# S5 products by lag with operands exchanged, four tiles in four column groups and one transposition back; VectorE's scans ahead of the pads of lags

## The chip, the cores and the metric

One core of one Trainium2 chip runs the whole program. The metric is the device time of one execution in microseconds, and the time of a kernel is the median of its runs. TensorE does matrix products, VectorE and ScalarE elementwise work (both read PSUM), GpSimd elementwise work in SBUF, SyncE issues most transfers.

## The reference

The reference is one inference step of a two-layer trunk, for a prompt of 256 tokens and 8 single tokens. Layer 0 is gated linear attention with a short convolution and a dense SwiGLU; layer 1 is an S5 state-space mixer and a mixture of eight experts. The edited code belongs to the S5 mixer:

```python
u = (h @ w_in).reshape(bsz, t, S5_GROUPS, S5_GROUP)        # 64 groups of 16 channels
bu = einsum('btgi,gpi->btgp', u, bb)                       # complex, 64 states a group
x_t = ab * x_{t-1} + bu_t                                  # for each group and state
y = einsum('gip,btgp->btgi', c_re, x_re) - einsum('gip,btgp->btgi', c_im, x_im) + d_skip * u
```

Everything is float32.

## The kernel before

Every engine has its own list of instructions, written out by hand, and runs it in order; semaphores tie the lists together. The S5 mixer takes four time steps as one, so that the recurrence runs over 64 chunks (`CHUNKS`) of 4 steps. Two groups fill 128 partitions with their 2 x 64 states, and such a pair is one of 32 pairs; the kernel works on 4 pairs at a time, in 8 tiles `k` of 4 pairs `r`. Within a chunk the output of one step from the input of an earlier one needs only the product of C, A to the power of the lag, and B: a 16x16 matrix for each group and each lag 0 to 3. These are the products by lag.

For each tile `k`:

- ScalarE's `pad_b` (L1097) lays the 4 lags of B of each pair in `b_pad`, 128 partitions (2 groups x 64 states) by 128 columns (4 lags x 2 groups x 16 inputs), with zeros where state and input belong to different groups.
- TensorE's `turns_of_b` (L2238) transposes the 8 blocks (4 pairs, real and imaginary) into banks 6 and 7, and ScalarE's `b_mats` (L1119) copies them out.
- TensorE's `lag_products` (L2248) multiplies, for each pair, `b_pad` as the stationary operand with C (`c_now`, 16 columns) as the moving one, real and imaginary part into one sum: bank 3 then holds 128 rows (lag, group, input) by 16 outputs for each pair.
- VectorE's `lags` (L1714) masks this into `k_pad` (L1720) and adds the skip term in four small instructions (L1725); ScalarE's `k_mats` (L1126) spreads it into `k_mat`.
- TensorE's `chunk_sums` (L2258) makes the input of the recurrence, `turn_back` (L1693) on VectorE and two additions on GpSimd (L786, L787) rotate it, `scans` (L1730) runs it over the chunks with two scan instructions, and `rotate_im` (VectorE) and `rotate_re` (GpSimd, L769) rotate back.
- GpSimd's `pad_c` (L757) pads C, `sample_states` (L1138) and `last_states` (L1147) copy states on ScalarE.
- TensorE's `outputs` (L2270) sums `k_mat` times the input and padded C times the states into bank 4, and ScalarE's `gelu` (L1154) takes it out.

The four lists run these steps of different tiles in a loop over `k`. TensorE: transposes of tile k+1, outputs of tile k-2, products by lag and chunk sums of tile k+1. VectorE: `turn_back` of k, `lags` of k+1, `scans` and `rotate_im` of k-1. GpSimd: decay and additions of k, `pad_c` of k, `rotate_re` of k-1. ScalarE: `b_mats` of k+1, `pad_b` of k+2, `sample_states` and `k_mats` of k, `last_states` of k-1, `gelu` of k-2. `pad_c` and `k_mats` of a tile write into buffers that `outputs` two tiles earlier still reads, so they wait for it. In the first rounds and near the end TensorE also makes pieces of the modulation (`ada`, L1975): products of 32 stationary columns (`csT`) and 512 moving ones, in four column groups of the array, which write to four quarters of the partitions.

All products go through one helper, `mm` (L1938), so in the profile they carry line 1939 and are told apart by their operands: products by lag read `arena,plain_hi`, chunk sums `arena,plain_lo` in 16 passes, outputs `arena,plain_lo` and `plain_parts,plain_hi` in turn. A float32 product is two MATMUL records. Transposes are line 2245.

Of the kernel before, what the change touches and what calls it, by code (L numbers as in the profile page):

```python
# [7 lines left out]
ALU = mybir.AluOpType  # L8
ACT = mybir.ActivationFunctionType
# [5 lines left out]
P = 128  # L15
D = 1024
KT = D // P
# [105 lines left out]
def hybrid_trunk(nc, x_prompt, x_sample, c_prompt, c_sample, state_gla, state_conv, state_s5_re, state_s5_im,  # L123
# [11 lines left out]
    with ExitStack() as ctx:  # L135
# [5 lines left out]
        def sem(name):  # L141
            return ctx.enter_context(nc.semaphore(name))
# [49 lines left out]
        def shaped(flat, shape):  # L192
            if len(shape) == 2:
                return flat.rearrange("p (a b) -> p a b", b=shape[1])
            if len(shape) == 3:
                return flat.rearrange("p (a b c) -> p a b c", b=shape[1], c=shape[2])
            return flat
# [8 lines left out]
        def bview(ap, shape, *dims):  # L206

            for d in dims:
                ap = ap.unsqueeze(d)
            return ap.broadcast_to(shape)  # L210
# [65 lines left out]
        b_mat = [shaped(x[:, 0:1024], (2, 4, P)) for x in mats]  # L276
        k_mat = [shaped(x[:, 1024:1536], (4, 4, QUAD)) for x in mats]
        k_pad = [shaped(x[:, 1536:1664], (4, QUAD)) for x in mats]
        work = [shaped(plain_parts[:, 1024 * i:1024 * i + 1024], (4, 4, CHUNKS)) for i in range(2)]
        x_in = [shaped(plain_parts[:, 2048 + 584 * i:2632 + 584 * i], (2, 4, CHUNKS + NS + 1)) for i in range(2)]  # L280
        decay = [shaped(plain_parts[:, 3216 + 256 * i:3472 + 256 * i], (4, CHUNKS)) for i in range(2)]
# [3 lines left out]
        def two(at, *shape):  # L285
# [81 lines left out]
            sem(n) for n in ("steps_ready", "c_now_ready", "turns_ready", "table_ready", "table_saved",  # L367
                             "cos_loaded", "sin_loaded", "u_cleared", "k_cleared",
                             "u_first", "u_second"))
        b_pad_ready, c_pad_ready, tr_full, b_mat_ready, k_full, k_pad_ready, k_mat_ready = (  # L370
            sem(n) for n in ("b_pad_ready", "c_pad_ready", "tr_full", "b_mat_ready", "k_full", "k_pad_ready",
                             "k_mat_ready"))
        w_full, w_used, w_ready, z_ready, xre_ready, xim_ready, xs_ready, y_full, y_used, y_moved = (
            sem(n) for n in ("w_full", "w_used", "w_ready", "z_ready", "xre_ready", "xim_ready", "xs_ready", "y_full",
# [488 lines left out]
        def _(act):  # L863
# [233 lines left out]
            def pad_b(k):  # L1097

                if k >= 2:
                    act.wait_ge(tr_full, k - 1)  # L1100
                    act.wait_ge(k_full, k - 1)
                for i in range(2):
                    for g in range(2):
                        ins = act.activation(b_pad[k % 2][:, i, :, :].rearrange("q r (s g i) -> q (r s) g i", g=2, i=16)[:, :, g, :],
                                             b_steps[i][:, 4 * k:4 * k + 4, :, :].rearrange("q r s i -> q (r s) i"),
                                             ACT.Copy, scale=half_rows[:, g:g + 1])
                ins.then_inc(b_pad_ready, 1)
# [11 lines left out]
            def b_mats(k):  # L1119

                act.wait_ge(tr_full, k + 1)
                for i in range(2):
                    ins = act.activation(b_mat[k % 2][:, i, :, :].rearrange("q r p -> q (r p)"), bank[6 + i][:, :], ACT.Copy)
                ins.then_inc(b_mat_ready, 1)

            def k_mats(k):  # L1126

# [31 lines left out]
                act.activation(y_one[:, k, :, :], out[:, :, 0:NS], ACT.Gelu_apprx_tanh).then_inc(y_used, 1)  # L1159

            b_mats(0)
            act.wait_ge(acc_full, TILES["in1"] + KT)
            pad_b(1)
            for k in range(KT + 2):
                if k + 1 < KT:
                    b_mats(k + 1)
                if k + 2 < KT:
                    pad_b(k + 2)
                if k in (1, 2):
                    act.wait_ge(u_cleared, 1)  # L1170
                    for s_ in range(4):
                        act.activation(*place(slice(4, 8), k + 1, s_), ACT.Copy)
                    for at, s_ in ((0, 0), (CHUNKS + NS, 3)):
                        ins = act.activation(u_in[QUAD * s_:QUAD * s_ + QUAD, 4:8, k + 1, at:at + NS],
                                             uT[QUAD * (k + 1):QUAD * (k + 1) + QUAD, 4:8, TP:T], ACT.Copy)
                    if k == 2:
                        ins.then_inc(u_second, 1)
                if k < KT:
                    sample_states(k)
                    k_mats(k)  # L1180
                if k < 3:
                    ada(17 + k)
                if 1 <= k <= KT:
                    last_states(k - 1)
                if k >= 2:
                    gelu(k - 2)
                if k == KT:
                    ada(20)
                    split_dense_hi(act, 42)
# [121 lines left out]
        def _(dve):  # L1311
# [3 lines left out]
            def step(ins):  # L1315

                count[0] += 1
                ins.then_inc(v_step, 1)
                dve.wait_ge(v_step, count[0])
# [394 lines left out]
            def lags(k):  # L1714


                dve.wait_ge(k_full, k + 1)
                if k >= 2:
                    dve.wait_ge(k_mat_ready, k - 1)
                step(dve.tensor_tensor(k_pad[k % 2].rearrange("q r (g o) -> q r g o", g=2),  # L1720
                                       bview(bank[3][:, 0:64].rearrange("q (r o) -> q r o", r=4), [P, 4, 2, 16], 2),
                                       bview(group_mask[:, :], [P, 4, 2, 16], 1, 3), ALU.mult))
                last = k_pad[k % 2][96:P, :, :]
                for r in range(4):
                    ins = dve.scalar_tensor_tensor(out=last[:, r, :], in0=ident[96:P, 96:P],  # L1725
                                                   scalar=d_col[96:P, 4 * k + r:4 * k + r + 1], in1=last[:, r, :],
                                                   op0=ALU.mult, op1=ALU.add)
                ins.then_inc(k_pad_ready, 1)
# [9 lines left out]
            def rotate_im(k):  # L1738

                wk, x = work[k % 2], x_in[k % 2][:, 1, :, NS + 1:]  # L1740
                dve.wait_ge(z_ready, 2 * k + 2)
                if k >= 2:
                    dve.wait_ge(y_full, k - 1)
                    dve.wait_ge(last_copied, k - 1)
                dve.tensor_tensor(x, turn_sin[:, k, :, :], wk[:, 0, :, :], ALU.mult)
                step(dve.tensor_tensor(wk[:, 3, :, :], turn_cos[:, k, :, :], wk[:, 2, :, :], ALU.mult))
                dve.tensor_tensor(x, x, wk[:, 3, :, :], ALU.add).then_inc(xim_ready, 1)

            lags(0)
            for k in range(KT + 1):  # L1750
                if k < KT:
                    turn_back(k)
                if k + 1 < KT:
                    lags(k + 1)
                if k:
                    scans(k - 1)
                    rotate_im(k - 1)
                if 1 <= k <= 3:
                    mod_rows(16 + k)
                if k >= KT - 1:  # L1760
                    dve.wait_ge(y_used, 4)
                    for r in (2 * k - 14, 2 * k - 13):
                        for s_ in range(4):
                            dve.tensor_copy(*from_chunks(slice(0, 4), r, s_))
# [168 lines left out]
        def _(pe):  # L1933
# [4 lines left out]
            def mm(out, lhsT, rhs, start, stop):  # L1938
                return pe.matmul(out, lhsT, rhs, start=start, stop=stop, skip_group_check=True)  # L1939
# [307 lines left out]

            def lag_products(k):  # L2248

                if k:  # L2250
                    pe.wait_ge(k_pad_ready, k)
                for r in range(4):
                    for i in range(2):
                        ins = mm(bank[3][:, 16 * r:16 * r + 16], b_pad[k % 2][:, i, r, :], c_now[:, i, 4 * k + r, :],
                                 i == 0, i == 1)
                ins.then_inc(k_full, 1)

            def chunk_sums(k):  # L2258

                pe.wait_ge(b_mat_ready, k + 1)  # L2260
                pe.wait_ge(*((u_first, 1) if k < 4 else (u_second, 2)))
                if k:
                    pe.wait_ge(w_used, k)
                n = CHUNKS + NS
                for i in range(2):
                    for r in range(4):
                        ins = mm(bank[1 + i][:, n * r:n * r + n], b_mat[k % 2][:, i, r, :], u_in[:, k, r, NS:], True, True)
                ins.then_inc(w_full, 1)
# [17 lines left out]
            turns_of_b(0)  # L2286
            lag_products(0)
            chunk_sums(0)
            for k in range(KT + 2):
                if k + 1 < KT:  # L2290
                    turns_of_b(k + 1)
                if k >= 2:
                    outputs(k - 2)
                if k + 1 < KT:
                    lag_products(k + 1)
                    chunk_sums(k + 1)
                if 1 <= k <= 3:
                    ada_rows(16 + k)
                if k < 3:
                    ada(17 + k)  # L2300
                if k == KT:
                    ada(20)
# [231 lines left out]
```

## Time and profile before

| | |
|---|---|
| median of 3 runs | 1842.84 us (1841.28 to 1846.24) |
| profiled execution | 1847.72 us, span 1845.9 us, mean granted clock 0.943 |
| busy share of the span | TensorE 94%, VectorE 75%, ScalarE 65%, GpSimd 8% |
| chain that ended last | TensorE 84%, VectorE 6%, issue 4%, DMA 3%, GpSimd 1%, ScalarE 2% |
| the S5 rounds with the edited code | about 506 to 637 us of the span |

How it is read: times are microseconds from the start of the span. A busy time counts an engine's own instructions; PEld is TensorE's loading of stationary operands, which overlaps PE. The clock is the share of full speed that was granted to TensorE: 1.00 is 2.4 GHz, 0.50 is 1.2 GHz. In an answer, `out<-in` names the memory written and read; `plain_hi`, `plain_lo`, `plain_parts` and `arena` are areas of SBUF, `bank` is PSUM. What stands in brackets at the end of a row is how long the engine was idle before it and what ended that. Ends of matmuls are modelled.

### The profile page before, as it was taken

How to read it: one execution, taken by the hardware profiler on the slowest of the kernel's cores; microseconds unless marked ns; L12 is line 12 of the kernel's file. 1: busy time of each engine (PE TensorE's matmuls, PEld its weight loads, DVE VectorE, ACT ScalarE, POOL GpSimd, SP SyncE). 2: the span in 40 equal slices, each digit the busy share in tenths (PEclk: the TensorE clock that was granted, in tenths of full speed). 3: DMA queues.
4: the chain of work that ended last, by engine and by line, in shares of the span. 5: the costliest groups of instructions: out<-in, count | busy, mean ns of one | idle time of the engine just before them, and what ended most of it. 6: DMA issues, size and time to landing. Idle time of an engine off the chain costs nothing.

```text
span 1845.9 us, 27103 instructions
## 1 busy us (share of the span) xinstructions
PE 1734.2 (94%) x9191; PEld 1457.0 (79%) x9191; DVE 1379.5 (75%) x1579; ACT 1201.8 (65%) x1491; POOL 146.4 (8%) x199
## 2 busy tenths in 40 slices
PE   6988899998899797999999999999999999999994
PEld 3877799986779695887887878878878788788884
DVE  3564445491643736998998989989989899899997
ACT  3623355303463445878888888888888888888885
POOL 1041000000044300700000000000000000000001
PEclk8988999999865698999999999999999999999997
DMA  8662654335630249998998989989989899899995
GB/s 349 257 258 90 237 194 160 141 151 194 289 137 1 103 178 382 399 418 323 422 367 348 410 312 419 392 325 420 360 358 400 314 422 380 343 412 355 399 376 197
DMA packets 72903, 553.49 MB, mean 300 GB/s; under 512 B 8256, under 2 KB 8527, under 8 KB 15328
## 3 DMA queue, kind: packets, MB, share of 16 engines
q1 hardware_dynamic: 69186, 538.54, 73.9%
q0 software_dynamic: 3072, 12.54, 1.8%
q10 hardware_dynamic: 542, 1.20, 0.2%
q8 instruction: 43, 0.70, 0.1%
q14 instruction: 60, 0.49, 0.1%
HBM read 530.74 MB, written 21.53 MB: 299 GB/s over the span
## 4 chain that ended last, share of the span: by engine, by line
PE 84%; DVE 6%; issue 4%; DMA 3%; ACT 2%; POOL 1%; ACTq 0%; DVEq 0%; POOLq 0%; SPq 0%
PE bank L1939 81%; PE bank L2406 1%; DMA ring<-in_dense_rows_dram 1%; DVE w_lo L516 1%; DMA arena<-in_state_conv_dram 1%; DVE arena L1686 1%; ACT w_hi L511 1%; DVE sq L1364 0%; PE bank L2385 0%; DVE rstd L1346 0%; ACT w_hi L463 0%; DVE w_lo L469 0%; DMA fT<-y_rows,row_i 0%; DVE sq L1517 0%; DVE arena L1899 0%
## 5 line engine op out<-in xcount | busy, mean ns | idle before, releaser
L1939 PE MATMUL bank<-w_hi,parts 128*128 128x512 f32 x3024 | 899.0, 392 | 14.8 <-DVE w_lo L516 13.3
L516 DVE TENSOR_TENSOR w_lo<-ring,w_hi 128x1024 fp32r<-128x1024 f32 x654 | 782.4, 1221 | 81.1 <-PE bank L1939 29.8
L511 ACT ACTIVATE w_hi<-ring 128x1024 fp32r<-128x1024 f32 x654 | 690.7, 1062 | 157.4 <-PE bank L1939 157.3
L1939 PEld LDWEIGHTS bank<-w_hi,parts 128*128 128x128 f32 x3024 | 561.6, 188 | 134.1 <-DVE w_lo L516 18.6
L1939 PE MATMUL bank<-w_lo,parts 128*128 128x512 f32 x1512 | 548.3, 390 | 0.0
L1939 PE MATMUL bank<-parts,w_hi 128*128 128x264 f32 x1600 | 312.6, 297 | 21.9 <-DVE parts L1353 21.9
L1939 PEld LDWEIGHTS bank<-w_lo,parts 128*128 128x128 f32 x1512 | 283.9, 188 | 60.3
L1939 PEld LDWEIGHTS bank<-parts,w_hi 128*128 128x128 f32 x1600 | 260.6, 198 | 33.9 <-issue 21.5
L1939 PE MATMUL bank<-parts,w_lo 128*128 128x264 f32 x800 | 234.0, 293 | 0.0
L469 DVE TENSOR_TENSOR w_lo<-ring,w_hi 128x2048 fp32r<-128x2048 f32 x50 | 114.5, 2295 | 148.2 <-ACT w_hi L463 148.2
L1939 PEld LDWEIGHTS bank<-parts,w_lo 128*128 128x128 f32 x800 | 158.0, 198 | 0.0
L511 ACT ACTIVATE w_hi<-hT 128x1024 fp32r<-128x1024 f32 x108 | 114.5, 1061 | 36.5 <-PE bank L1939 36.4
L886 ACT ACTIVATE arena<-bank 128x264 f32<-128x264 f32 (+2 forms) x89 | 34.6, 390 | 156.1 <-PE bank L1939 156.1
L516 DVE TENSOR_TENSOR w_lo<-hT,w_hi 128x1024 fp32r<-128x1024 f32 x108 | 131.1, 1220 | 5.4
L463 ACT ACTIVATE w_hi<-ring 128x2048 fp32r<-128x2048 f32 x50 | 95.1, 1908 | 8.0 <-PE bank L1939 5.3
L1939 PE MATMUL bank<-arena,ring 128*128 128x264 f32 x352 | 81.7, 395 | 6.1 <-DMA ring<-in_dense_rows_dram 6.1
L857 POOL DMA_INDIRECT arena<-y_rows,row_i x4 | 3.8, 942 | 1045.1 <-DMA y_rows<-arena 1044.2
L1939 PEld LDWEIGHTS bank<-arena,ring 128*128 128x128 f32 x352 | 68.3, 195 | 19.4 <-issue 7.3
L898 ACT ACTIVATE sq<-bank 128x264 f32<-128x264 f32 x16 | 6.2, 390 | 82.3 <-PE bank L1939 82.3
L1939 PE MATMUL bank<-ring,csT 128*32 128x512 f32 x384 | 56.5, 710 | 2.6 <-DMA ring<-in_dense_rows_dram 2.6
L1939 PE MATMUL bank<-arena,plain_lo 128*128 128x72 f32 x192 | 42.5, 374 | 10.1 <-ACT arena L1159 10.1
L1875 DVE TENSOR_TENSOR parts<-bank,parts 128x512 fp32r<-128x512 f32 x63 | 43.1, 684 | 8.2 <-ACT parts L1258 8.2
(412 smaller groups left out, 1289.4 us busy)
## 6 DMA issues: line engine op xcount, KB each, us to landing
ring<-in_expert_rows_dram SPq DMA_DIRECT2D x330, 1024.0 KB, 7.2
ring<-in_dense_rows_dram SPq DMA_DIRECT2D x48, 2048.0 KB, 8.3
hT<-in_expert_rows_dram SPq DMA_DIRECT2D x55, 1024.0 KB, 7.2
ring<-in_dense_rows_dram SPq DMA_DIRECT2D x8, 1408.0 KB, 6.4
x_rows<-arena SPq DMA_DIRECT2D x1, 7168.0 KB, 28.8
y_rows<-arena SPq DMA_DIRECT2D x10, 512.0 KB, 6.6
arena<-x_rows SPq DMA_DIRECT2D x9, 512.0 KB, 8.1
ring<-in_dense_rows_dram SPq DMA_DIRECT2D x2, 1024.0 KB, 4.8
```

The source lines that it names most:

```text
L463: act.activation(hi, raw, ACT.Copy).then_inc(hi_ready, 1)
L469: dve.tensor_tensor(lo, raw, hi.bitcast(F32), ALU.subtract).then_inc(lo_ready, 1)
L511: act.activation(hi_slots[u % AHEAD], raw_unit(u), ACT.Copy).then_inc(hi_ready, 1)
L516: dve.tensor_tensor(lo_slots[u % AHEAD], raw_unit(u), hi_slots[u % AHEAD].bitcast(F32), ALU.subtract).then_inc(lo_ready, 1)
L857: pool.indirect_dma_start(to, None, y_rows, bass.IndirectOffsetOnAxis(row_i[0:rows, i, b:b + 1], 0))\
L886: act.activation(out, tile_bank(tile[0])[0:rows, 0:n], func, **more).then_inc(acc_free, 1)
L898: act.activation(sq[:, k, :], src, ACT.Square).then_inc(sq_ready, 1)
L1686: dve.tensor_copy(*place(ks, r, s_))
L1875: dve.tensor_tensor(h_t[c % 2][1], bank[6][:, :], h_t[c % 2][0].bitcast(F32), ALU.subtract)\
L1939: return pe.matmul(out, lhsT, rhs, start=start, stop=stop, skip_group_check=True)
L2406: ins = pe.transpose(bank[6][:, P * q:P * q + P], h_act[:, c % 2, P * q:P * q + P], ident[:, :])
```

## The change

The products by lag exchange their operands: C of two neighbouring pairs (2 x 16 = 32 columns) is stationary, and `b_pad` (128 columns) moves. Each of the 4 pairs `r` writes to its own quarter of bank 3's partitions, so that its product stands in its own column group of the array; of the 32 rows written, 16 belong to pair `r` and 16 to its neighbour's C, which are not used. The result is the transpose of what it was. So ScalarE copies it out of PSUM (`copy_lags`) into a new area `lag_rows`, TensorE transposes it back with one transposition (`turn_lags`) into other columns of bank 3, and VectorE's `lags` reads it there, in two instructions of half the size, since of every two neighbouring blocks it takes the first for even and the last for odd pairs. In TensorE's order the products by lag of tile k+1 now stand ahead of the outputs of tile k-2, and the turning back behind the chunk sums. In VectorE's order `scans` and `rotate_im` of tile k-1 now stand ahead of `lags` of tile k+1.

```diff
+        lag_rows = [x[:, 1664:1792] for x in mats]
...
 def pad_b(k):
     if k >= 2:
         act.wait_ge(tr_full, k - 1)
-        act.wait_ge(k_full, k - 1)
+        act.wait_ge(lag_full, k - 1)
...
+def copy_lags(k):
+    act.wait_ge(lag_full, k + 1)
+    if k >= 2:
+        act.wait_ge(k_full, k - 1)
+    act.activation(lag_rows[k % 2], bank[3][:, 0:P], ACT.Copy).then_inc(lag_copied, 1)
...
             b_mats(0)
+            copy_lags(0)
...
                 if k + 1 < KT:
                     b_mats(k + 1)
+                    copy_lags(k + 1)
                 if k + 2 < KT:
                     pad_b(k + 2)
...
 def lags(k):
     dve.wait_ge(k_full, k + 1)
     if k >= 2:
         dve.wait_ge(k_mat_ready, k - 1)
-    step(dve.tensor_tensor(k_pad[k % 2].rearrange("q r (g o) -> q r g o", g=2),
-                           bview(bank[3][:, 0:64].rearrange("q (r o) -> q r o", r=4), [P, 4, 2, 16], 2),
-                           bview(group_mask[:, :], [P, 4, 2, 16], 1, 3), ALU.mult))
+    for pair in range(2):
+        of_pair = bank[3][:, P + 64 * pair:P + 64 * pair + 64].rearrange("q (x o) -> q x o", o=16)[:, 0:4:3, :]
+        ins = dve.tensor_tensor(k_pad[k % 2][:, 2 * pair:2 * pair + 2, :].rearrange("q r (g o) -> q r g o", g=2),
+                                bview(of_pair, [P, 2, 2, 16], 2),
+                                bview(group_mask[:, :], [P, 2, 2, 16], 1, 3), ALU.mult)
+    step(ins)
...
                 if k < KT:
                     turn_back(k)
-                if k + 1 < KT:
-                    lags(k + 1)
                 if k:
                     scans(k - 1)
                     rotate_im(k - 1)
+                if k + 1 < KT:
+                    lags(k + 1)
...
 def lag_products(k):
     if k:
         pe.wait_ge(k_pad_ready, k)
-    for r in range(4):
-        for i in range(2):
-            ins = mm(bank[3][:, 16 * r:16 * r + 16], b_pad[k % 2][:, i, r, :], c_now[:, i, 4 * k + r, :],
-                     i == 0, i == 1)
-    ins.then_inc(k_full, 1)
+    for i in range(2):
+        for r in range(4):
+            pair = c_now[:, i, 4 * k + r // 2 * 2:4 * k + r // 2 * 2 + 2, :].rearrange("q t o -> q (t o)")
+            ins = mm(bank[3][QUAD * r:QUAD * r + QUAD, 0:P], pair, b_pad[k % 2][:, i, r, :], i == 0, i == 1)
+    ins.then_inc(lag_full, 1)
+
+def turn_lags(k):
+    pe.wait_ge(lag_copied, k + 1)
+    pe.transpose(bank[3][:, P:2 * P], lag_rows[k % 2], ident[:, :]).then_inc(k_full, 1)
...
             turns_of_b(0)
             lag_products(0)
             chunk_sums(0)
+            turn_lags(0)
             for k in range(KT + 2):
                 if k + 1 < KT:
                     turns_of_b(k + 1)
+                    lag_products(k + 1)
                 if k >= 2:
                     outputs(k - 2)
                 if k + 1 < KT:
-                    lag_products(k + 1)
                     chunk_sums(k + 1)
+                    turn_lags(k + 1)
```

## Rows read from the trace of the kernel before

**Rows 1.** Busy time of each engine by stretch (instructions), clock, DMA share, GB/s.
```profile
512.87:563.03 50.16, 49.11 (x280) 39.69 (x281) 23.71 (x66) 29.64 (x79) 23.76 (x29) 0.64 0.34 126
563.03:606.92 43.89, 40.07 (x186) 39.15 (x186) 17.71 (x47) 14.35 (x47) 19.82 (x24) 0.50 0.00 0
```

**Rows 2.** Waits from 505 to 637 us: total, times, longest.
```profile
DVE plain_lo L1720 <- PE bank L1939: 47.1, 7, 9.7
...
PE bank L1939 <- ACT arena L1159: 10.1, 5, 5.2
```

**Rows 3.** Chain that ended last, one round: start, us, what.
```profile
592.32 8.70 PE bank L1939 x40
...
601.05 0.30 DVE plain_lo L1720
...
602.16 1.29 DVE plain_parts L1735 x2
...
603.52 0.97 POOL plain_parts L776
...
606.21 0.21 ACT arena L1151
...
606.92 5.38 PE bank L1939 x24
```

**Rows 4.** Timeline of one late round: start, us, engine, instruction, count.
```profile
582.87 3.53 PE L1939 MATMUL bank<-arena,plain_hi 128*128 128x16 f32 x16
583.16 1.04 POOL L763 TENSOR_TENSOR plain_hi<-plain_hi,half_rows 128x512 f32<-128x512 f32 x1 [2.97 <-PE bank L1939]
...
586.24 3.67 PE L1939 MATMUL bank<-arena,plain_lo 128*128 128x72 f32 x16
...
589.70 1.92 PE L2245 MATMUL bank<-ident,plain_hi 128*128 128x128 f32 x8
...
592.07 1.09 ACT L1123 ACTIVATE plain_lo<-bank 128x512 f32<-128x512 f32 x2
```

**Rows 5.** Timeline of the early rounds, columns as in rows 4.
```profile
512.87 3.60 PE L1939 MATMUL bank<-arena,plain_hi 128*128 128x16 f32 x16 [0.27 <-DVE plain_lo L1725]
...
514.18 0.32 DVE L1709 TENSOR_TENSOR arena<-arena,bank 128x32 f32<-128x32 f32 x2
...
524.98 1.86 PE L1939 MATMUL bank<-arena,plain_hi 128*128 128x16 f32 x16
...
549.83 0.41 PE L1939 MATMUL bank<-arena,plain_lo 128*128 128x72 f32 x2 [1.05 <-ACT arena L1159]
```

**Rows 6.** Stretches by granted clock, columns as in rows 1.
```profile
511.04:524.69 13.65, 13.38 (x62) 9.88 (x61) 7.22 (x26) 5.29 (x15) 6.94 (x9) 0.50 0.06 13
524.69:528.10 3.41, 3.41 (x33) 3.41 (x31) 1.16 (x6) 2.87 (x7) 0.46 (x1) 1.00 0.78 308
...
534.90:541.75 6.85, 6.85 (x64) 6.85 (x62) 1.66 (x6) 6.27 (x16) 2.38 (x3) 1.00 0.83 307
```

**Rows 7.** Timeline around one piece of the modulation.
```profile
517.64 2.34 PE L1939 MATMUL bank<-arena,plain_lo 128*128 128x72 f32 x10
...
519.91 3.64 PE L1939 MATMUL bank<-ring,csT 128*32 128x512 f32 x16
...
520.76 0.20 PEld L1939 LDWEIGHTS bank<-ring,csT 128*32 128x32 f32 x4 [0.66 <-issue]
...
521.62 0.20 PEld L1939 LDWEIGHTS bank<-ring,csT 128*32 128x32 f32 x4 [0.66 <-issue]
...
523.48 0.48 PE L2245 MATMUL bank<-ident,plain_hi 128*128 128x128 f32 x1
```

**Rows 8.** Groups by line and shape, 563.03 to 606.89 us: busy us, mean ns.
```profile
L1158 ACT ACTIVATE arena<-bank 128x256 f32<-128x256 f32 x3 | 1.1, 367 | 0.0
...
L1709 DVE TENSOR_TENSOR arena<-arena,bank 128x32 f32<-128x32 f32 x6 | 0.9, 199 | 0.0
...
L1159 ACT ACTIVATE arena<-bank 128x32 f32<-128x32 f32 x3 | 0.6, 189 | 0.0
```

More of the change, by code:

```diff
@@ L369, in hybrid_trunk @@
                              "u_first", "u_second"))
-        b_pad_ready, c_pad_ready, tr_full, b_mat_ready, k_full, k_pad_ready, k_mat_ready = (
-            sem(n) for n in ("b_pad_ready", "c_pad_ready", "tr_full", "b_mat_ready", "k_full", "k_pad_ready",
+        b_pad_ready, c_pad_ready, tr_full, b_mat_ready, lag_full, lag_copied, k_full, k_pad_ready, k_mat_ready = (
+            sem(n) for n in ("b_pad_ready", "c_pad_ready", "tr_full", "b_mat_ready", "lag_full", "lag_copied", "k_full", "k_pad_ready",
                              "k_mat_ready"))
```

## The prediction

> **What bounds the kernel now.** I read the stage in which the edited lines run, by stretches, by waits, along the chain and instruction by instruction, in that order. The stretches say where TensorE is the limit: from 512.87 to 563.03 us it is busy 49.11 of 50.16 us, and from there to 606.92 us it is busy 40.07 of 43.89 us at the lower of its two clock levels, 1.2 GHz (granted 0.50) [rows 1]. The waits say who suffers: VectorE waits 47.1 us in seven pieces for TensorE before the first instruction of `lags` (L1720), and TensorE 10.1 us in five pieces for the gelu of ScalarE (L1159) [rows 2].
>
> The chain joins the two into a loop of 14.6 us that repeats once per tile of four groups [rows 3]: TensorE 8.70 us (`outputs`, then the products by lag), VectorE's pads from 601.05, its scans from 602.16, GpSimd's `rotate_re` from 603.52, ScalarE's `last_states` and gelu from 606.21, and TensorE again at 606.92. The scans need nothing from the products by lag; they only stand behind `lags` in VectorE's order. So one tile's scan waits for the next tile's products, and these wait behind `outputs`.
>
> What TensorE pays is a price per pass, not per column. A float32 product is two passes: 16 passes with 16 moving columns take 582.87 to 586.24, 16 with 72 columns take 586.24 to 589.70 [rows 4], together 6.83 us for 32, or 0.213 us each at 1.2 GHz, 0.107 at 2.4 GHz (the 16 passes of a tile in the stretch from 524.69 at granted 1.00 take 1.86 us with their tail [rows 5, 6]). What both have in common is 128 stationary columns.
>
> **The change part by part.**
>
> *Products by lag.* Before: 8 products, 16 passes of 128 stationary and 16 moving columns, 3.41 us at 1.2 GHz, 1.71 at 2.4. After: the same 16 passes with 32 stationary and 128 moving columns, in four column groups. The nearest rows are the modulation's products, in the same four groups with 512 moving columns: 16 passes, which start in waves of four, the third weights 0.86 us after the second (520.76, 521.62) [rows 7], at granted 0.50 [rows 6]. A wave of 512 columns in 0.855 us makes 0.213 us with 128, so four waves are 0.85 us. Entering and leaving the groups costs a little: ten passes from 517.64 would end at 519.77 and the modulation starts at 519.91, 0.14 us later; its four waves end at 519.91 + 3.42 = 523.33 and the transposes start at 523.48, 0.15 us later [rows 7]. So a tile costs 0.85 + 0.29 = 1.15 us at 1.2 GHz. At 2.4 GHz the waves are 0.43; the two switches lie between 0.15 and 0.30, I take 0.20, so 0.63. Bounds: four waves without switches (0.85) and no overlap at all (3.41 + 0.29 = 3.70).
>
> The Trainium skill (TensorE: Matmul & The Clock Gate, Part 3, measured speedups) puts three column tiles at 2.38 times instead of 3. The rows show whole waves of four; by the page's ratio a wave would take 0.27 instead of 0.213 us, and the sum below would be some 1.5 us smaller.
>
> *Turning back.* ScalarE's copy of 128x128 out of PSUM lies between its copies of 128x32 and 128x256, 0.19 and 0.37 us [rows 8]; I take 0.28. TensorE's transposition is one pass, 0.21 us at 1.2 GHz, 0.11 at 2.4. It waits for the copy, and behind it in TensorE's order stand the next tile's transposes and everything after. But the copy follows `b_mats`, done some 1.5 us after the transposes before it (589.70 + 1.92 = 591.62; `b_mats` 592.07 to 593.16 [rows 4]), while TensorE comes to the transposition only after products by lag, outputs and chunk sums, 1.15 + 5.12 + 3.41 = 9.7 us after those transposes. ScalarE would have to be 8 us late, so I cost the wait at nothing.
>
> *Pads of lags.* One VectorE instruction of 128x128 (0.30 us in the chain [rows 3]) becomes two of half the size; a small one out of PSUM, 128x32, is 0.20 us [rows 8]. So `lags` grows from 1.11 (601.05 to 602.16 [rows 3]) by between 0 and 0.3 us; I take 0.2. TensorE hides this: from the turning back to the next products by lag it has nine passes, 1.92 us, and the answer comes after 0.21, a pass's tail of 0.16 (582.87 + 3.53 against 586.24 [rows 4]) and 1.31 of `lags`, 1.7 us. At 2.4 GHz that cover is gone, and TensorE would wait about 0.6 us.
>
> *Scans ahead.* `scans` and `rotate_im` of the tile before now follow `turn_back` at once, and `rotate_re` no longer waits for them. VectorE is busy 17.71 of 43.89 us [rows 1], so there is room. What is late next on that side is GpSimd: `pad_c` waits for `outputs` and `rotate_re` stands behind it. That loop is 5.12 (outputs) + 0.29 to its start (582.87 to 583.16) + 2 x 1.04 [rows 4] + 2.69 (603.52 to 606.21) + 0.71 (to 606.92) [rows 3] = 10.9 us.
>
> *Three late rounds (563.03 to 606.92).* TensorE alone now needs 24 + 16 + 1 + 8 = 49 passes, 10.45 us, and 1.15 for the products by lag: 11.6 us, more than GpSimd's 10.9. Two rounds become 11.6; the third has neither transposes nor products by lag behind it and falls to GpSimd's 10.9. From 43.9 to 34.1: 9.8 us. If GpSimd and VectorE slow each other, 1 us a round less; if every round falls to GpSimd's loop, 1.4 more.
>
> *Early rounds (512.87 to 563.03).* TensorE is full, so its passes count one for one where nothing else is late. Tiles 1 to 4 had 3.41 + 1.71 + 1.71 + 3.41 = 10.2 us of products by lag. Now tiles 1 to 5 stand here, 1.15 + 0.63 + 0.63 + 1.15 + 1.15, with four turnings back of 0.64 in all: 5.35. That is 4.9 us less. The idle 1.05 us at 549.83, for a gelu behind a table load, is filled by tile 4's products, which now stand ahead of that wait [rows 5]: 5.9. Tile 1's chunk sums wait for `turn_back`, which ended at 514.50 and comes 0.2 later, where TensorE would be free at about 514.2 [rows 5]: 5.4. Other engines may be late in places I can't see; I take 5.0, bounds 2.5 and 6.
>
> *Before 512.87 and after 606.92.* Before it TensorE waits for VectorE anyway [rows 5]. After it there are no products by lag, and `scans` already stands first. Nothing in either.
>
> *The clock.* It stands at 2.4 GHz for 3.41 us from 524.69, a little after the modulation's 512-column passes, and falls after a stretch that holds tile 2's products with 16 moving columns; it comes up again for 6.85 us from 534.90 [rows 6]. With 128 columns in that place it may hold for another stretch after each of three such blocks. A stretch of 3.41 us at 2.4 GHz does up to 6.8 us of the same passes, so the bounds are 0 and 10 us; I take 2, near the rows in which it fell again.
>
> Sum: 9.8 + 5.0 + 2 = 16.8 us. The profiled execution took 1847.72 us (span 1845.9), so it would take 1830.9. The median of the three runs, 1842.84, is 4.9 us lower: 1826.0 us.
>
> **The rivals.**
>
> *(a) The clock stays up.* If the denser passes hold 2.4 GHz through most of the stage, a late round is no longer TensorE's but GpSimd's at 2.56 + 0.29 + 2.08 + 2.69 + 0.71 = 8.3 us: 9 us less than above in the three rounds, and some 7 less in the early half, where the clock is at 0.64 on average [rows 1]; 2 of these 16 are counted already. Time: 1812. For it: the clock rose after dense passes. Against it: it is at 0.50 through all the late rounds, which hold transposes with 128 columns too. The Trainium skill (same page, Part 4) says that transposes in that mode don't bring the full clock. By that rule the added turning back does nothing for it; the trace, where it rose 1.2 us after the transposes had begun [rows 6, 7], can't tell them from the modulation before.
>
> *(b) The groups don't overlap.* If short passes run in turn, a tile costs 3.70 + 0.21 us against 3.41, and a late round of TensorE is 10.45 + 3.70 = 14.2 instead of 14.6. Left are 0.4 + 0.4 + 3.7 of the rounds by the scans, less 0.5 in each of tiles 1 to 4 and plus 1 for the idle gap: 3.5 us, 1839. Against it: the waves of four [rows 7].
>
> *(c) Slower: the turning back waits.* One mechanism: ScalarE reaches the copy late, TensorE stands at the transposition, and transposes, products by lag and outputs of the next tile stand behind it. It decides from 8 us of delay on ScalarE; the change loses when each of seven tiles waits over 16.8 / 7 = 2.4 us beyond that. At 3.5 us the time is 1842.8 - 16.8 + 24.5 = 1850.5. ScalarE is busy 14.35 of 43.89 us in the late rounds [rows 1], so only the early ones, where it also copies the stage's inputs, could show it.
>
> **How the numbers follow.** The forecast 1826 has 0.70, its own range 1820 to 1833; (a) 0.15; (b) 0.10; (c) 0.05. The range from 1814 to 1838 takes in most of (a) and the near side of (b). A change under 0.3%, 5.5 us, can't be told from none here: faster means below 1837.3, slower above 1848.4. The forecast lies below that nearly whole (0.69), (a) whole, (b) for a third: 0.87 faster; 0.09 the same; 0.04 slower.
>
> **What would show it.** In the changed profile: products by lag of about 1.1 us a tile with 32 stationary columns; start to start of `outputs` in the late rounds 11 to 12 us with TensorE nearly without idle time; the 47.1 us wait at L1720's successor still long, since VectorE has time, but nothing behind it on the chain; `rotate_re` right behind `pad_c`. It is wrong if the products by lag still take over 3 us, if TensorE idles over 1 us before the turning back, or if the late rounds stay over 13 us.

## The result and the profile after

The changed kernel takes 1811.12 us (median of 4 runs, 1809.64 to 1812.09), the kernel before 1844.54 us beside it (1841.28 to 1847.88): ratio 0.9819 [0.9803, 0.9835]. The gain of 33.4 us is twice the 16.8 us forecast, and the time lies below the range. The profiled executions differ by 38.0 us of span (1845.9 and 1807.9), and lie in it as follows:

| piece of the span | before | after | difference | forecast |
|---|---|---|---|---|
| up to the S5 stage | 505.9 | 502.8 | -3.1 | 0 |
| to the products by lag of tile 1 | 7.0 | 7.1 | +0.1 | 0 |
| early rounds, to `outputs` of tile 2 | 50.4 | 43.1 | -7.2 | -5.0 |
| three late rounds | 43.7 | 31.6 | -12.1 | -9.8 |
| rest of the stage | 30.7 | 30.2 | -0.5 | 0 |
| from there to the first expert job | 202.9 | 205.2 | +2.3 | 0 |
| seven turns of the loop over expert jobs | 846.7 | 829.6 | -17.1 | 0 |
| last turn and end | 158.7 | 158.3 | -0.4 | 0 |

The clock had a term of its own, 2 us, for the whole stage. The four lines of the stage make -19.7 us, so that part came out near its 16.8. The other large piece is in a loop that the diff doesn't touch.

**The stage.** Stretches of the changed kernel from the products by lag of tile 1 to `outputs` of tile 2 and to the end of the third late round (columns as in [rows 1]):

```profile
509.90:553.04 43.14, 37.98 (x300) 30.02 (x300) 27.55 (x74) 30.26 (x83) 25.65 (x30) 0.76 0.40 147
553.04:584.63 31.59, 28.12 (x176) 26.48 (x172) 19.30 (x46) 14.39 (x49) 19.84 (x24) 0.61 0.00 1
```

They answer to [rows 1]: the granted clock rose from 0.64 to 0.76 and from 0.50 to 0.61. A full late round on the chain, and the same round in the timeline:

```profile
552.10 9.75 PE bank L1952 x56
561.85 0.21 PE bank L2275
562.07 1.71 PE bank L2258 x8
563.77 9.75 PE bank L1952 x56
```

```profile
560.51 0.73 POOL L777 TENSOR_TENSOR plain_parts<-fT,plain_parts 128x256 f32<-128x256 f32 x1
...
561.65 0.42 PE L2275 MATMUL bank<-ident,plain_lo 128*128 128x128 f32 x1
...
561.86 1.92 PE L2258 MATMUL bank<-ident,plain_hi 128*128 128x128 f32 x8
...
562.10 0.36 DVE L1732 TENSOR_TENSOR plain_lo<-bank,group_mask 128x64 f32<-128x64 f32 x2 [6.69 <-PE bank L2275]
562.50 1.16 DVE L1738 SCALAR_TENSOR_TENSOR plain_lo<-ident,arena,plain_lo 32x32 f32<-32x32 f32 x4
...
563.71 1.08 PE L1952 MATMUL bank<-plain_hi,arena 128*32 128x128 f32 x16
...
564.72 0.50 PEld L1952 LDWEIGHTS bank<-arena,plain_lo 128*128 128x128 f32 x2 [0.38 <-issue]
```

The round that was passed from engine to engine [rows 3] is now TensorE's alone, 11.67 us from 552.10 to 563.77 (forecast 11.6). The products by lag take 1.01 us from their first pass to the first of `outputs` (563.71 to 564.72) where they took 3.37 (582.87 to 586.24 [rows 4]). GpSimd's `rotate_re` (560.51) starts before the pads of lags (562.10) instead of after them.

**The jobs.** The next two fences are one turn of the loop over expert jobs, before and after (columns as in [rows 1]):

```profile
851.49:972.60 121.11, 118.71 (x540) 97.70 (x539) 108.95 (x101) 98.56 (x103) 0.00 (x0) 1.00 0.94 374
```

```profile
820.00:938.55 118.55, 118.55 (x541) 98.21 (x540) 110.15 (x102) 98.61 (x103) 0.00 (x0) 1.00 0.98 382
```

Both at full clock, with the same TensorE work; but before, TensorE was idle for 2.40 us of this turn (1.58 to 2.40 us in each of the seven, 13.3 us in all), and the turns took 120.5 to 121.5 us against 118.5. The eighth job, behind which the loop does not turn again, took 118.5 us in both kernels. VectorE at the turn, before and then after:

```profile
852.48 0.68 DVE L1899 COPY arena<-bank 128x512 f32<-128x512 f32 x1
857.94 1.23 DVE L516 TENSOR_TENSOR w_lo<-ring,w_hi 128x1024 fp32r<-128x1024 f32 x1 [4.78 <-PE bank L1939]
861.14 2.36 DVE L516 TENSOR_TENSOR w_lo<-ring,w_hi 128x1024 fp32r<-128x1024 f32 x2 [1.98 <-PE bank L1939]
```

```profile
832.00 0.69 DVE L1912 COPY arena<-bank 128x512 f32<-128x512 f32 x1
833.71 1.22 DVE L517 TENSOR_TENSOR w_lo<-ring,w_hi 128x1024 fp32r<-128x1024 f32 x1 [1.03 <-ACT w_hi L512]
```

The copy is the last work of a job and the subtraction the first of the next. Between them VectorE stood 4.78 us, later 1.98 us more, and now 1.03. The page puts the wait down to TensorE, but TensorE itself was waiting for these subtractions, 0.85 and 1.55 us at the turn:

```profile
859.22 0.73 PE L1939 MATMUL bank<-w_hi,parts 128*128 128x512 f32 x2 [0.85 <-DVE w_lo L516]
...
862.42 0.73 PE L1939 MATMUL bank<-w_hi,parts 128*128 128x512 f32 x2 [1.55 <-DVE w_lo L516]
```

On the chain of the kernel before, the time behind the copy is "issue", time in which VectorE waited for nothing that the profile shows (start, us, what):

```profile
853.16 4.55 issue
```

What comes at these gaps is a transfer of instructions. The DMA view of the same two turns, before and after (queue, kind: packets, MB, share):

```profile
q14 instruction: 5, 0.04, 0.1%
```

```profile
q14 instruction: 1, 0.01, 0.0%
```

Before, the packets lie at 852.44, 855.73, 859.19 and 861.94 us, around the two gaps, and at 916.76. Each lasts some 0.3 us, so most of a gap lies around the packets, and no view shows what fills it. The whole page has 60 of them before and 25 after. The Trainium skill (Runtime: NRT & Kernel Launch, Instruction fetch mechanics) says that an engine holds two blocks of instructions and that a branch taken to one outside them waits for a DMA. The trace agrees in what it can show, packets and gaps at the turn; how much the engine holds it doesn't show. From this comes theory F: the eight instructions that the change adds to VectorE's list, one more for each tile's pad, shifted its loop over jobs against the blocks, and this alone is the 17.1 us.

### The profile page after: what moved, and what is told of

Read it like the earlier page. It is cut to its first block, busy times and chain, and to the rows that moved or that the text cites. A ratio compares the mean times of both kernels' runs of the same rounds, so it can differ in the third digit from the quotient of the medians.

```text
span 1807.9 us, 27141 instructions
## 1 busy us (share of the span) xinstructions
PE 1704.9 (94%) x9199; PEld 1433.0 (79%) x9199; DVE 1390.2 (77%) x1587; ACT 1201.8 (66%) x1499; POOL 147.0 (8%) x199
## 4 chain that ended last, share of the span: by engine, by line
PE 88%; DVE 5%; ACT 3%; DMA 3%; issue 1%; POOL 1%; ACTq 0%; DVEq 0%; POOLq 0%; SPq 0%
PE bank L1952 85%; PE bank L2427 2%; DMA ring<-in_dense_rows_dram 1%; DMA arena<-in_state_conv_dram 1%; DVE arena L1696 1%; DVE sq L1374 0%; DVE sq L1503 0%; PE bank L2406 0%; DVE rstd L1356 0%; ACT w_hi L464 0%; DVE sq L1527 0%; DVE w_lo L470 0%; PE bank L2258 0%; DMA fT<-y_rows,row_i 0%; ACT hT L1203 0%
## 5 line engine op out<-in xcount | busy, mean ns | idle before, releaser
L1952 PEld LDWEIGHTS bank<-arena,ring 128*128 128x128 f32 x352 | 68.5, 195 | 18.7 <-issue 6.7
L1952 PE MATMUL bank<-ring,csT 128*32 128x512 f32 x384 | 52.4, 665 | 2.6 <-DMA ring<-in_dense_rows_dram 2.6
L1952 PE MATMUL bank<-arena,plain_lo 128*128 128x72 f32 x192 | 40.2, 357 | 14.4 <-ACT arena L1167 12.1
L1952 PEld LDWEIGHTS bank<-arena,plain_lo 128*128 128x128 f32 x192 | 35.9, 267 | 18.6 <-issue 16.8
```

## The experiments

Theory F, against the rival that something in the new S5 part lets the jobs run faster, was tested from both sides. Theory S (scans ahead and exchange both needed for the short rounds) was tested by doing one part alone, and the clock by doubling the new products. In the table the ratio is to the kernel before in the same session, with its 95% interval (its median was 1843.0 us beside e1 to e4, 1843.7 beside e5 to e8, 1845.8 beside e9 to e11). Every kernel's stage is from the end of the last dense product to the first gated one; "half" is the time in it at granted 0.50, in one profile each; "late rounds" go from the first product of `outputs` to that of the next tile; "turn" is a job's.

| kernel | median us (runs) | ratio | stage | half | late rounds | turn |
|---|---|---|---|---|---|---|
| before | 1844.5 | 1 | 131.7 | 102.7 | 14.5, 14.6, 14.6 | 121.0 |
| e1 before, pad split | 1821.0 (4) | 0.9859 [0.9824, 0.9894] | 125.1 | 85.7 | 14.7, 14.7, 14.7 | 118.5 |
| e6 before, 12 fewer | 1825.2 (2) | 0.989 [0.986, 0.992] | 126.3 | 90.3 | 14.3, 14.4, 14.4 | 118.5 |
| e3 scans ahead only | 1831.1 (5) | 0.9917 [0.9889, 0.9946] | 114.7 | 68.5 | 10.4, 10.4, 8.7 | 120.9 |
| e4 exchange only | 1825.4 (4) | 0.9888 [0.9854, 0.9922] | 126.1 | 76.6 | 15.0, 15.0, 15.0 | 118.5 |
| after | 1811.1 (4) | 0.9819 [0.9803, 0.9835] | 112.0 | 65.8 | 11.7, 11.6, 8.3 | 118.5 |
| e2 after, 8 fewer | 1832.8 (5) | 0.9931 [0.9899, 0.9963] | 111.9 | 65.8 | 11.7, 11.7, 8.3 | 121.1, one 125.8 |
| e5 scans ahead, pad split | 1818.2 (4) | 0.9839 [0.9798, 0.988] | 126.1 | 97.0 | 13.6, 13.6, 11.9 | 118.5 |
| e11 the same again | 1813.2 (6) | 0.9836 [0.9805, 0.9867] | 110.9 | 58.0 | 13.6, 8.1, 8.6 | 118.5 |
| e8 e5, `rotate_re` first | 1811.1 (4) | 0.9808 [0.9782, 0.9834] | 112.0 | 65.9 | 10.4, 10.4, 8.7 | 118.5 |
| e7 after, `rotate_re` first | 1808.9 (4) | 0.9803 [0.9781, 0.9825] | 108.3 | 62.1 | 11.7, 11.7, 5.9 | 118.5 |
| e9 after, products twice | 1801.2 (4) | 0.9753 [0.9734, 0.9772] | 105.9 | 46.0 | 8.5, 8.6, 10.0 | 118.5 |
| e10 e7, products twice | 1799.5 (4) | 0.9745 [0.9726, 0.9764] | 101.0 | 34.3 | 7.4, 9.1, 6.1 | 118.5 |

**The place of the loop.** e1 is the kernel before with the pad in two; e2 the changed kernel without the skip term of one pair in four, so that VectorE's list has its old length; e6 the kernel before with 12 skip terms left out.

```diff
 # e1
-                step(dve.tensor_tensor(k_pad[k % 2].rearrange("q r (g o) -> q r g o", g=2), ...))
+                for pair in range(2):
+                    ins = dve.tensor_tensor(k_pad[k % 2][:, 2 * pair:2 * pair + 2, :].rearrange("q r (g o) -> q r g o", g=2),
...
 # e2
-                for r in range(4):
+                for r in range(3):
 # e6
-                for r in range(4):
+                for r in range(2 if k < 4 else 3):
```

> The kernel before, with VectorE's pad instruction of each tile split into two halves: 8 VectorE instructions more, nothing else changed. Theory F (fetch): the 17 us that left the expert jobs (121 to 118.5 us a job) come from where the turn of VectorE's loop over jobs lies in its instruction stream, which 8 instructions more shift. Then jobs of 118.5 us, about 25 instead of 60 fetches on queue 14, and about 1827 us in all, with the S5 rounds still at 14.6 us. Rival D (data): the jobs got shorter because the stage before ends earlier and the transfers fall into another phase. Then jobs stay at 121 us and the time at 1844 us.

> The changed kernel with three instead of four of the small VectorE instructions per tile that add the skip term: 8 VectorE instructions fewer, as many as before; the skip term of every fourth pair is left out. Theory F: the loop lies again as before, jobs of 121 us, about 60 fetches on queue 14, S5 rounds as in the changed kernel, 1811 + 17 = 1828 us. Rival D: jobs of 118.5 us, 1811 us or 1 us less.

> The kernel before with 12 of the 32 small VectorE instructions that add the skip term left out (so the skip term of those pairs is missing). Theory F (place of the loop against fetch blocks): VectorE's loop over jobs has 269 instructions; it costs 2.5 us a turn where it touches one block more, which 8 more instructions end. Moved 12 the other way it lies wholly ahead of the same boundary: jobs of 118.5 us, about 25 fetches on queue 14, about 1822 us. Rival M (more instructions help, by a delay or by data): with fewer instructions jobs stay at 121 us, 60 fetches, 1843 us.

VectorE at the turn of the loop, in e1 and then in e2:

```profile
842.98 0.68 DVE L1901 COPY arena<-bank 128x512 f32<-128x512 f32 x1
844.68 2.36 DVE L516 TENSOR_TENSOR w_lo<-ring,w_hi 128x1024 fp32r<-128x1024 f32 x2 [1.02 <-ACT w_hi L511]
```

```profile
835.01 0.68 DVE L1912 COPY arena<-bank 128x512 f32<-128x512 f32 x1
840.15 1.23 DVE L517 TENSOR_TENSOR w_lo<-ring,w_hi 128x1024 fp32r<-128x1024 f32 x1 [4.46 <-PE bank L1952]
```

The stall goes with eight added instructions in the old S5 part and comes back with eight fewer in the new one; the pages have 25 and 60 instruction packets. In e6 it goes with 12 fewer: what counts is the place, and not that more instructions help. F holds, the rivals D (data) and M (more instructions help) fall; the times themselves were some us off (1821.0 for 1827, 1832.8 for 1828, 1825.2 for 1822).

**One part alone.** e3 moves only the scans, e4 keeps the exchange and puts `lags` back ahead of them. e3 and before have the loop at the costly place, e4 and e1 at the cheap one.

```diff
 # e3 (on before; e4 is the reverse, on the changed kernel)
-                if k + 1 < KT:
-                    lags(k + 1)
                 if k:
                     scans(k - 1)
                     rotate_im(k - 1)
+                if k + 1 < KT:
+                    lags(k + 1)
```

> The kernel before with only VectorE's order changed: scans and rotate_im of tile k-1 ahead of lags of tile k+1; products by lag as before. As many VectorE instructions as before, so theory F: jobs of 121 us. Late S5 rounds: TensorE's 64 passes, 13.7 us instead of 14.6, the last of three at GpSimd's 10.9, some 4 to 6 us less in the stage, 1839 us. If the clock is what gives the changed kernel its short rounds, it stays at 0.50 here. Rival D: jobs shorter too, 1822 us.

> The changed kernel with VectorE's order as before (lags ahead of scans). As many VectorE instructions as the changed kernel, so theory F: jobs of 118.5 us. Late S5 rounds: outputs 5.12, chunk sums 3.41, turning back and tail 0.4, lags 1.3, scans 1.3, rotate_re 2.7, last states and gelu 0.7: 14.9 us, no gain; the early rounds some 4 us less. 1844 - 17 - 4 = 1823 us. Rival D: jobs at 121 us, 1840 us.

The exchange alone does not pay: its rounds stay at 15.0 us, since the loop through VectorE and GpSimd is not broken, and it stands 4.4 us above e1. Of the 4.7 us between the two profiled spans (1823.4 and 1818.7) only 1.0 lies in the stage, so the rest is not shown to be the exchange's. The scans alone give 11.9 us (1843.0 to 1831.1). e3's rounds missed the expected 13.7: two of them took 10.4 us, since TensorE's clock came up in between, with 68.5 us at 0.50 in the stage against 65.8 in the changed kernel. So theory S falls: short rounds, and a clock that comes up, are there without the exchange. Put at the cheap place with the split pad (e5), its rounds were 13.6:

> The kernel before with the pad instruction split in two (8 VectorE instructions more, as in the changed kernel) and scans ahead of lags, products by lag as before. It stands beside the changed kernel with the same place of VectorE's loop, so the difference is what the exchange of operands gives. Theory G (GpSimd bounds): once the scans go ahead and the clock comes up for part of the stage, the rounds are GpSimd's loop of 10.5 us and TensorE's shorter products buy nothing: 1809 us, within 3 us of the changed kernel's 1811. Rival T (TensorE bounds): the exchange saves over 2 us in each of seven tiles: 1821 us or more.

```profile
563.28 1.06 PE L1941 MATMUL bank<-plain_parts,plain_hi 128*128 128x72 f32 x4
...
567.98 3.53 PE L1941 MATMUL bank<-arena,plain_hi 128*128 128x16 f32 x16
...
576.84 1.06 PE L1941 MATMUL bank<-plain_parts,plain_hi 128*128 128x72 f32 x4
```

64 passes of 0.213 us fill the round, in a stretch at 0.50 of 68.3 us. But e5's runs go from 1811 to 1827. Hence the repetition, e11, from the same text:

> The kernel of e5 once more (operands as before the change, scans ahead of lags, the pad in two so that VectorE's loop over jobs stands as in the changed kernel), in more rounds, beside e9 and e10 on one chip. Its runs were from 1811 to 1827. If the exchange is worth only what it takes off the rounds at 1.2 GHz (13.6 to 11.7 us, two or three rounds, 4 to 6 us), the median stays 4 to 8 us above the changed kernel's 1811 and the runs spread again over 10 us or more. If e5's upper runs were the chip's and not the kernel's, the runs agree within 4 us near 1811 and the exchange is worth nothing at equal place.

Its six runs are 1807 to 1814 four times and 1824 twice; with e5, six of ten lie at 1807 to 1814 and four at 1824 to 1827. The profiles of the two groups differ in the clock: 97.0 us at 0.50 (e5) and 58.0 us (e11); over all ten the mean granted clock is 0.943 or 0.944 in the four and 0.950 to 0.956 in the six. Neither expectation of e11 came true: its median is 2.0 us above the changed kernel's, and its runs spread over 17 us. All four runs of the changed kernel lie within 2.5 us, which are too few to say that it never takes the longer course. So beside the scans the exchange is worth nothing to be seen in the better runs and, if the changed kernel has no such runs, 13 to 16 us in the others.

Another pair at equal place stands in the table: e3 and e2 both have the scans ahead and the loop at the costly place. Without the exchange the median is 1831.1 us, with it (and eight skip terms fewer) 1832.8; the stage of the profile is 114.7 and 111.9 us. A few us in the stage are all that the exchange shows there, and nothing in the whole.

**GpSimd's order.** The forecast had `rotate_re` behind a waiting `pad_c` as the next limit. e7 (on the changed kernel) and e8 (on e5) turn them round:

```diff
-                    pad_c(k)
                 if k:
                     rotate_re(k - 1)
+                if k < KT:
+                    pad_c(k)
```

> The changed kernel with GpSimd's rotate_re of tile k-1 ahead of pad_c of tile k. Theory G: rotate_re then doesn't stand behind pad_c, which waits for outputs, so GpSimd leaves the loop; rounds are TensorE's 11.6 us at 0.50 and 7 to 8 us where the clock is up, and the clock falls less since TensorE idles less: stage 100 to 107 instead of 112 us, 1799 to 1806 us. Rival T: late rounds bound by TensorE at 0.50 alone: stage 111 to 112, 1811 us.

> Scans ahead, pad split in two, products by lag as before, and GpSimd's rotate_re ahead of pad_c. Here TensorE has 64 passes a round, 13.7 us at 0.50 and 6.9 at 1.00. Theory G: as with GpSimd's old order or some us less, 1800 to 1809 us; with TensorE now the bound the exchange of operands should show: the kernel with it 3 to 8 us faster than this one. Rival T: 1821 us, as with GpSimd's old order.

The third late round falls from 8.3 to 5.9 us, so this was its limit. The whole, 0.9803 [0.9781, 0.9825], is not apart from the changed kernel's, and 1808.9 us misses the 1799 to 1806 expected. e8 and e7 are a third pair that differs in the exchange alone: 1811.1 and 1808.9 us, 2.2 apart where 3 to 8 were expected, with stages of 112.0 and 108.3.

**The clock.** Do the exchanged products have to do with it? e9 issues them twice, e10 does so in e7:

```diff
+                for again in range(2):
                     for i in range(2):
                         for r in range(4):
```

> The changed kernel with the products by lag of each tile issued twice into the same bank (the second sum starts anew and gives the same values): 16 more passes of 128 moving columns in four column groups per tile, nothing else. Theory D (the exchanged products, being dense, are what brought TensorE's clock up in the stage, half-speed time 102.7 to 65.8 us): twice as many bring it up earlier or hold it longer; the half-speed time falls below 50 us, the late rounds go from 11.7 towards GpSimd's 8.7, the stage stays at or below 112 us, the median at or below 1811. Rival R (the course of the clock is set by the rest of the stage, the exchange only shortens the passes): the half-speed stretches stay as they were, each tile costs four more waves of 0.213 us at 1.2 GHz or half of that at 2.4 GHz: late rounds 11.7 + 0.85 = 12.5, the stage 112 + 8 x 0.43 to 0.85 = 116 to 118 us, the median 1815 to 1817.

> The kernel of e7 (the changed one with GpSimd's rotate_re ahead of pad_c) with the products by lag of each tile issued twice, as in e9. Theory D: with GpSimd's loop at 7.1 to 8.3 us nothing else holds a round back, so a clock that comes up earlier shows fully: late rounds under 9, half-speed time under 45 us instead of 62, stage under 105 us, median under 1806. Rival R: rounds 11.7 + 0.85 = 12.5, stage 112 to 115 us, median 1812 to 1815.

Stretches of the changed kernel by its clock, then of e9 (columns as in [rows 1]):

```profile
518.25:538.70 20.45, 17.52 (x185) 12.92 (x178) 18.38 (x42) 19.08 (x48) 16.21 (x18) 1.00 0.70 255
538.70:576.25 37.55, 36.45 (x203) 34.37 (x203) 16.01 (x47) 18.41 (x59) 18.18 (x22) 0.50 0.07 31
576.25:583.10 6.85, 4.91 (x45) 4.60 (x41) 6.75 (x14) 2.69 (x10) 5.86 (x6) 1.00 0.00 0
583.10:603.60 20.50, 13.76 (x64) 10.99 (x64) 17.91 (x35) 3.99 (x17) 10.26 (x13) 0.50 0.01 2
```

```profile
519.90:543.80 23.90, 21.01 (x251) 16.50 (x247) 19.16 (x42) 22.55 (x57) 16.20 (x18) 1.00 0.71 265
543.80:554.00 10.20, 10.20 (x74) 9.39 (x72) 5.48 (x16) 4.45 (x16) 6.78 (x8) 0.50 0.01 2
554.00:571.10 17.10, 13.56 (x165) 12.69 (x165) 13.29 (x32) 10.63 (x36) 11.80 (x14) 1.00 0.00 1
571.10:598.40 27.30, 20.59 (x99) 18.70 (x102) 21.97 (x45) 6.30 (x27) 15.88 (x18) 0.50 0.00 1
```

With 128 passes more in the stage, TensorE is busy for less of it: 85.50 us against 91.13. The long stretch at 0.50 that holds two of the late rounds is cut from 37.55 to 10.20 us, while the one behind it grows from 20.50 to 27.30. The first late round in e9 (8.5 us, the second 8.6) has TensorE idle again before the products:

```profile
558.37 1.04 PE L2258 MATMUL bank<-ident,plain_hi 128*128 128x128 f32 x8
561.00 1.08 PE L1952 MATMUL bank<-plain_hi,arena 128*32 128x128 f32 x32 [1.59 <-DVE plain_lo L1738]
```

That is the wait for the pads; the forecast gave it 0.6 us at 2.4 GHz, and here it is 1.59. The four small instructions of `lags` (L1738) took 1.98 us there, against 1.16 in the round of the changed kernel shown above; why is not shown.

Doubled products do what theory D of e9 and e10 (dense products) expected of them, but for e10's second late round (9.1 us instead of under 9), and its rival (1815 to 1817 and 1812 to 1815) falls. The other half of theory D, that the exchanged products are what brought the clock up in the changed kernel, is not borne out: e3 and e8 don't have them, and their stages have 68.5 and 65.9 us at 0.50 against its 65.8. e10 has the lowest median of the study, and its interval, like e9's, lies apart from the changed kernel's; it does a part of its work twice, and gains by the clock.

## Why the prediction was wrong

**The step that failed** is "Before 512.87 and after 606.92 … Nothing in either." I looked for work that the change adds or moves there, found none, and did not ask what the length of an engine's list does to a loop behind it. Eight added VectorE instructions were worth 17.1 us in the profile. By medians each of two pairs that differ in the place lies 22 us apart (before and e1, 1843.0 and 1821.0; e2 and after, 1832.8 and 1811.1). In the profiles of the first pair 17.1 us are the jobs, 6.6 are in the stage, where e1 had 85.7 us at 0.50 and before 102.7, and 2.8 ahead of it. In those of the second the jobs make 23.1 us, with one e2 turn of 125.8 us among them, and 3.0 us lie ahead of the stage. Only the 17 us of the jobs are shown to be the place's.

**The late rounds were right, the early ones by luck.** Two late rounds of TensorE alone at 1.2 GHz: 11.6 forecast, 11.68 and 11.65 measured between starts of `outputs`. The products by lag: 1.15 forecast, 1.01 measured at 0.50, 0.57 against 0.63 at 1.00. Waves of four column groups hold at 128 columns; rival (b) is out. The Trainium skill (TensorE: Matmul & The Clock Gate, Part 3, measured speedups) has three column tiles at 2.38 times; in the changed kernel the waves of four start 0.21 us apart at 0.50, so four whole waves of 0.213 us are 0.85 of the measured 1.01, and the trace doesn't show such a loss here. The early rounds came out at -7.2 us for -5.0, but that is no proof of their sum: e1, which has neither part of the change, took 43.5 us for them and e11, without the exchange, 42.4, against 43.1 in the changed kernel and 50.4 before; the mean granted clock over them is 0.75 or 0.76 in these three and 0.64 before.

**The turning back** costs one pass, 0.21 us on the chain, and no wait in the late rounds; rival (c) is out. The pads were mis-sized: `lags` took 1.56 us (562.10 to 563.66), not 1.31, so the cover of 1.92 us is just used up at 1.2 GHz. Waits for ScalarE's gelu remain, and VectorE's long wait at `lags` is shorter but harmless (window 502 to 622 us):

```profile
DVE plain_lo L1732 <- PE bank L2275: 27.0, 5, 9.3
...
PE bank L1952 <- ACT arena L1167: 12.1, 3, 5.2
```

They answer to [rows 2], 47.1 us in 7 pieces and 10.1 in 5.

**The clock was mis-sized.** I took 2 us within 0 to 10. The third late round, at 1.00, took 8.3 us, the 8.3 that rival (a) gave it, in place of 10.9. With the other terms as forecast, 14.8 us, the stage's 19.7 leave 4.9 for the clock. The mechanism was wrong too: the forecast hung this term on the 128 columns of the exchanged products, and the clock came up as much without them in e3 and e8, though not in e5. Rival (a) named nearly the right time, 1812, for the wrong reason: the clock did not stay up (65.8 us at 0.50).

**What the two parts are worth.** The forecast gave the exchange most of the gain: without shorter products, rival (b), it had 3.5 of the 16.8 us left. It held the clock at 0.50 in the late rounds, where TensorE's own time does count (13.6 us in e5, 11.7 after); but with the scans ahead alone the clock came up, rounds were 10.4 us, and the three late ones made 29.6 us (e3, e8) against 31.6 with the exchange. It is the scans ahead that break the loop: without them the exchange gains nothing (e4 against e1), and beside them it is worth -1.7 to 2.2 us in the median of two pairs, and 2 to 7 against the two series of e5 and e11, whose runs spread. By medians the two together are worth 9.9 us over e1 and 10.3 between before and e2; the 19.7 us of the profile contain 6.6 us that e1's stage has too. Why e1's clock differs from that of the kernel before isn't settled; that kernel itself ran from 1838.4 to 1853.2 us beside the experiments, with mean granted clocks of 0.942 to 0.949. The 3.1 us before the stage are not the change's, and their cause is open: e4 began it at 504.6 and e2 at 505.9, with the same work up to there as the changed kernel's 502.8, and e1 at 503.1 with that of the kernel before.

## What to carry to other kernels

Where an engine's list has a loop, count the instructions that a change puts ahead of it, and look at the instruction queues and at the first instruction after each turn: a few instructions more or fewer can add or take a stall per turn, so a variant is compared with another of the same loop place. In a ring of engines, first move what doesn't depend on the slow step out of its way; then ask what the engine's own time is. Where TensorE runs at either clock level, a change that alters its work may change the level of the rounds behind it, more than the work itself is worth.

## What had not been expected of the hardware

A turn of VectorE's loop with instruction packets around it cost VectorE a gap of 3.65 to 4.78 us and one of about 2.0, and TensorE 1.58 to 2.40 us of idle time, seven times in the run of the kernel before. The same program can run its stage with 58.0 or 97.0 us at the lower clock (e11, e5), 1807 to 1827 us in all. And 16 more passes of products a tile made the kernel 10 us faster (e9); what in them brought the clock up, their number, columns or place, these runs don't tell apart.
